# Bias lines replicated 16 times in DRAM instead of 128, and read by eight pairs of transfers onto every eighth partition

## The reference

```
s = einsum(q_blk, k) + rel_bias[rel_bucket(qpos[:, None] - kpos[None, :])]
s = where(qpos - kpos >= 0, s, -inf)
p = softmax(s)
```

## Time and profile before

| | us |
|---|---|
| median of 3 runs | 2331.86 (2328.55 to 2335.62) |
| the profiled execution | 2334.23 |
| its span | 2332.6 |
| TensorE busy | 2076.8 |
| VectorE busy | 1424.1 |
| POOL busy | 1017.5 |
| ScalarE busy | 871.6 |

### The profile page before, as it was taken

How to read it: one execution, slowest core, us unless ns; L and a number is a source line. 1 busy time by engine, 2 the same in 40 slices (tenths; PEclk the granted TensorE clock), 3 DMA queues, 4 the chain that set the end, 5 groups by cost and what they waited for, 6 DMA issues and landing times.

```text
span 2332.6 us, 24219 instructions
## 1 busy us (share of the span) xinstructions
PE 2076.8 (89%) x7378; PEld 1198.3 (51%) x7378; DVE 1424.1 (61%) x2980; ACT 871.6 (37%) x2116; POOL 1017.5 (44%) x1104
## 2 busy tenths in 40 slices
PE   7989999999999987898978998886999998878776
PEld 6768877778868643453423443342445444222222
DVE  3674464554477579774576654476846558684445
ACT  3544444645434332652223252223325223222222
POOL 0200000100000047677467566556755756777774
PEclk9999999999999899999999999998999999999999
DMA  8435545155545679999999999999999999999997
GB/s 315 171 124 174 190 161 205 50 190 180 180 145 185 271 319 409 344 396 412 414 410 409 416 411 412 411 414 396 401 415 387 413 413 409 410 409 409 409 410 310
DMA packets 172558, 752.66 MB, mean 323 GB/s; under 512 B 19184, under 2 KB 19472, under 8 KB 152864
## 3 DMA queue, kind: packets, MB, share of 16 engines
q0 software_dynamic: 148640, 544.05, 58.9%
q1 hardware_dynamic: 22224, 198.37, 22.7%
q10 hardware_dynamic: 1584, 8.91, 1.0%
HBM read 750.18 MB, written 4.22 MB: 323 GB/s over the span
## 4 chain that ended last, share of the span: by engine, by line
PE 49%; DMA 19%; DVE 12%; POOL 9%; issue 8%; ACT 2%; DVEq 1%; POOLq 0%; ACTq 0%; SPq 0%
PE ps L998 13%; DMA Z<-v,experts 10%; PE ps L731 8%; PE ps L733 8%; PE ps L732 8%; DMA Z<-u,experts 7%; PE ps L1018 6%; DVE Z L2039 5%; POOL Z L2413 4%; POOL Z L2428 3%; POOL ring L2428 1%; DMA ring<-panels 1%; PE ps L1075 1%; DVE ring_lo L1850 1%; DMA ring<-v,experts 1%
## 5 line engine op out<-in xcount | busy, mean ns | idle before, releaser
L998 PE MATMUL ps<-Z 128*128 128x512 f32 x1792 | 853.7, 622 | 157.8 <-DMA Z<-v,experts 95.4
L2039 DVE CUSTOM_DVE_ANT_0 Z<-Z,ps 128x1024 f32<-128x1024 f32 x512 | 612.0, 1219 | 408.6 <-DMA Z<-u,experts 402.1
L998 PEld LDWEIGHTS ps<-Z 128*128 128x128 f32 x1792 | 335.8, 197 | 635.4 <-issue 393.6
L2413 POOL DMA_INDIRECT Z<-u,experts x512 | 489.7, 956 | 293.0 <-issue 138.1
L2428 POOL DMA_INDIRECT Z<-v,experts x448 | 430.8, 962 | 252.0 <-PE ps L998 145.9
L1850 DVE TENSOR_TENSOR ring_lo<-ring,ring_hi 128x1024 fp32r<-128x1024 f32 x212 | 247.9, 1221 | 195.8 <-ACT ring_hi L1311 195.5
L1470 ACT ACTIVATE hdot<-hdot 128x4 f32<-128x4 f32 x128 | 26.3, 205 | 655.5 <-DVE hdot L2039 655.3
L731 PE MATMUL ps<-ring_hi,xT_lo 128*128 128x512 f32 x592 | 237.9, 402 | 14.2 <-DVE xT_lo L1909 8.9
L1018 PE MATMUL ps<-ring,o 128*128 128x512 f32 x528 | 232.3, 593 | 1.4 <-ACT o L1498 1.4
L732 PE MATMUL ps<-ring_lo,xT 128*128 128x512 f32 x592 | 232.9, 393 | 0.0
L733 PE MATMUL ps<-ring_hi,xT 128*128 128x512 f32 x592 | 232.7, 393 | 0.0
(11 more groups left out here) (285 smaller groups left out, 2152.0 us busy)
## 6 DMA issues: line engine op xcount, KB each, us to landing
ring<-panels SPq DMA_DIRECT2D x106, 1024.0 KB, 5.0
ring<-panels SPq DMA_DIRECT2D x37, 2048.0 KB, 10.4
Z<-u,experts POOLq DMA_INDIRECT x512, 12.1
Z<-v,experts POOLq DMA_INDIRECT x448, 12.8
Z<-panels SPq DMA_DIRECT2D x3, 2048.0 KB, 21.8
gain<-gains ACTq DMA_DIRECT2D x4, 1024.0 KB, 4.7
bias_lines<-bias_line POOLq DMA_DIRECT2D x1, 3072.0 KB, 13.8
gain<-gains ACTq DMA_DIRECT2D x5, 512.0 KB, 6.8
```

The costliest lines, as they stand in the source:

```text
L998: last = mm(ps[:, c, :], diag[s], vrow[s][:, c * NC:(c + 1) * NC], start=slot == 0, stop=slot == SLOTS - 1 or n == SUMMED[-1] - 1)
L2039: v.tensor_tensor_reduce(out=row, in0=row, in1=dotted, scale=1.0, scalar=0.0, op0=ALU.mult, op1=ALU.add, accum_out=hdot[:, t, slot:slot + 1])\
L2413: g.indirect_dma_start(out=urow[s], out_offset=None, in_=(u0, u1)[layer], in_offset=bass.IndirectOffsetOnAxis(ap=experts[:, t, slot:slot + ...
```

## The change

The replicated tensor has 16 copies instead of 128. Eight transfers of `later` and eight of `early` take the place of one each. Transfer number `at` fills partitions at, at + 8, ..., at + 120, sixteen of them, each from a copy of its own. The start of the source moves by one element with each `at`, and by eight from one of its partitions to the next. The waits count 256 instead of 32, since each transfer adds 16.

```diff
+COPIES = 16
...
-    lines_dram = nc.dram_tensor("bias_lines", (P, HEADS, LINE), F32).ap()
+    lines_dram = nc.dram_tensor("bias_lines", (COPIES, HEADS, LINE), F32).ap()
...
                 if call == 0:
-                    dve.wait_ge(lines_in, 32)
+                    dve.wait_ge(lines_in, 2 * 16 * P // COPIES)
...
                     pool.dma_start(lines_dram.rearrange("p h l -> p (h l)"),
-                                   bass.AP(line_dram.tensor, 0, [[0, P], [1, HEADS * LINE]])).then_inc(lines_out, 16)
+                                   bass.AP(line_dram.tensor, 0, [[0, COPIES], [1, HEADS * LINE]])).then_inc(lines_out, 16)
 
                     pool.wait_ge(lines_out, 32)
-                    later = bass.AP(lines_dram.tensor, P - 1, [[HEADS * LINE - 1, P], [LINE, HEADS], [1, SEQ]])
-                    early = bass.AP(lines_dram.tensor, 2 * P - 1, [[HEADS * LINE - 1, P], [LINE, HEADS], [1, P]])
-                    pool.dma_start(bias[:, :, P:S_COLS], later).then_inc(lines_in, 16)
-                    pool.dma_start(bias[:, :, 0:P], early).then_inc(lines_in, 16)
+                    for at in range(P // COPIES):
+                        steps = [[HEADS * LINE - P // COPIES, COPIES], [LINE, HEADS]]
+                        later = bass.AP(lines_dram.tensor, P - 1 - at, steps + [[1, SEQ]])
+                        early = bass.AP(lines_dram.tensor, 2 * P - 1 - at, steps + [[1, P]])
+                        pool.dma_start(bias[at::P // COPIES, :, P:S_COLS], later).then_inc(lines_in, 16)
+                        pool.dma_start(bias[at::P // COPIES, :, 0:P], early).then_inc(lines_in, 16)
...
-                    pool.wait_ge(lines_in, 32)
+                    pool.wait_ge(lines_in, 2 * 16 * P // COPIES)
                     pool.wait_ge(loaded, 16 * 3)
```

## The result

The changed kernel takes 2336.98 us (median of 22 runs, 2329.85 to 2343.15) against 2331.44 for the kernel before on the same chip (22 runs, 2328.48 to 2337.14). Forecast were 2328 us and a range of 2322 to 2334. The time is within the 0.3% called no change, but on the other side and outside the range. The profiled execution took 2338.71 us, with a span of 2337.1.

What follows compares the result with a forecast made beforehand. TensorE is busy 89% of the span, and from 950 us gathers fill the transfer engines; the change touches only the first 80 us. Terms 0 - 4.0 + 0 + 0 + 0 = -4.0 us gave 2327.9, range 2322 to 2334.

Steps and rivals of the forecast that it cites:

- Parts 1 and 3: POOL's start: replication lands after 4.5 us, sixteen bias reads issue from 37.4 us at 0.6 us each; 0.
- Rival B: POOL's queue delays the attention if an issue costs over 1.0 us: 2334.8 (chance 0.05), or serially 2360 (0.03).
- Part 5: The two changed waits, VectorE's for the bias and POOL's before staging: bias lands by 61, 11.8 us of cover; 0.
- small row: Last small transfer behind the bias reads in POOL's queue, whose landing frees POOL to stage; POOL forecast free at 61.
- Part 2: The late panel near 48 us: its halves land in time, so hole and lower clock behind it vanish; -4.0 us.
- old hole: TensorE's 2.14 us idle before the matmul at 50.50, waiting for a late panel; 4.02 us with the clock loss.
- higher row: The longer of two profiled landing times, 8.3 and 9.8 us, of panel halves beside the bias reads.
- Part 4: Moved reads lie over panel 3's second half and panel 4, which still lands with 2.8 and 1.3 us room; 0.
- queue model: Transfer engines' work from 37.4 us: reads at 332 GB/s take 9.5 us, 21.8 in all, through by 59.2.
- rival A: Narrow reads at half rate delay panel 4: hole of 2.7 us, 4.6 with clock; +0.6, 2332.5 us; chance 0.18.

Runs made afterwards that it cites:

- byhead128: Kernel before with its 128 copies, but sixteen bias reads, each of two heads onto all 128 partitions; 2333.25 us, ratio 1.0006.
- copies32: Changed kernel with 32 copies instead of 16, four pairs of reads onto partitions 4 apart; 2331.02 us (0.9998 of before), repeated 2332.38 (1.0012).
- changed_again: The changed kernel repeated unchanged for a second trace; 2333.42 us, ratio 1.0013 to the kernel before.
- three controls: The kernel before, unchanged, traced three more times; 2330.34 us (ratio 1.0007) for the first, then one execution each of 2329.28 and 2331.59.
- copies64: Changed kernel with 64 copies instead of 16, two pairs of reads onto every second partition; 2331.01 us (0.9999 of before), repeated 2331.26 (0.9994).

## Why the prediction was wrong

**Parts 1 and 3 were right.** Replication: 3.3 us to landing against 4.5; first bias read at 36.87 against 37.4, though the engine came 0.7 late to it. Issues: 0.56 against 0.6, with some luck: the number of runs, by which the step chose, doesn't set the time alone. byhead128's reads have the same 256 runs and take 0.73 to 0.76 us to issue. Rival B's own mechanism, an issue dearer than 1.0 us, did not occur. **Part 5 was right in what releases what**, with less room than given: VectorE's score work is released by TensorE, POOL's staging by TensorE, 1.7 us after the small row's landing instead of 11.8. The landings themselves were far off: the bias was due by 61 and came at 71.3, the small row at 75.1.

**Part 2 closed the old hole, but at a price from one execution.** TensorE has no idle time at 48 to 50 us. The step's term, -4.0, was 2.1 of hole and 1.9 of clock. Over six traces of kernels with 128 copies and wide reads the excess of that panel is 4.02, 2.34, 1.76, 1.85, 2.02 and 3.88, a mean of 2.6: behind holes of 1.4 to 2.1 us the clock fell in two of six. And of panel 3's second half the step said that it lands at the higher row, 9.8; it took 11.8, which ate the 1.2 us of room and left the hole of 0.73.

**Part 4 is the step that failed:** "Panel 4's halves, at 8.3 and 9.8, land at 54.1 and 58.3", so "0". They took 11.9 and 14.7, and the sign that the prediction names for being wrong, a new hole of over 1 us before 85 us, came true. The durations came from rows in which wide reads stood beside the panels, and the queue model from 332 GB/s; both held for copies32 (8.4 and 10.1 us for panel 4's halves) and byhead128 (8.5 and 9.5), neither for reads onto partitions 8 apart. With those the engines are as busy and pass a quarter to a third less. The new hole, 2.50 us and 4.50 with the clock, is the place and nearly the size that rival A named (2.7, and 4.6). The size has luck in it: by A's own terms the halves land at 45.83 + 15.6 = 61.4, not 62.3, which makes a hole of 1.8; they landed at 64.1. A alone would have been +0.6; its chance of 0.18 was too low, since the argument against it rested on rows of another kind of read.

The rule quoted with A, the Trainium skill (SBUF — State Buffer, section "Door 1: The DMA port swizzle"), agrees with the traces in order: partitions 4 apart and whole sets, which reach all 16 ports by it, pass 363 to 370 GB/s; 8 apart, 8 ports, 242 and 272; sixteen neighbours, 4 ports, 189. The rates hold the panels' own bytes too, so they are no clean halves and quarters, and no run wrote by ports alone.

**The balance.** At the first score work the changed kernel stands, as a mean of its two traces, at 86.2 us, and the kernel before, over its four, at 83.4: +2.8. That is the mean of 5.53 and 4.94 of new holes less 2.5 of old (four traces), 2.7. Behind the fourth staged pair come 0.9 more. Together +3.7, against +3.0 (0.13%, changed_again) and +4.4 (0.19%) in the timed runs. The stretch near 770 us isn't in that sum. By the traces it is 3.0 to 6.4 us longer in the changed kernel than in the three controls, but equal to before's own; timed runs carry no such marks, and both traced executions of the changed kernel were slower than its medians (2338.71 for 2336.98, 2339.59 for 2333.42), so how much of it is in the medians stays open.

Against the forecast of -4.0 the traces thus account for 7.6 us: 5.2 for the new holes that part 4 put at 0, 1.5 by which part 2 priced the old hole too high, 0.9 for the drain, which had no term. Measured were 8.4 and 7.0.

**What the forecast would have needed** was also not to be had from the hole alone. copies32 has it closed with no new one, scores start 3.2 us sooner (80.2 for 83.4), and its times are 0.9998 and 1.0012 of before: the attention gives back 0.4, the stretch near 770 us some 3. No version here beats the kernel before; the nearest, copies64, has 0.9999 and 0.9994 (0.9985 to 1.0003).

Not tried: reading the lines directly from the single one in DRAM, which needs a source that steps backwards.

## What to carry over

When copies are thinned out and a read becomes several strided ones, see which partitions each of them writes: reads onto 32 partitions 4 apart passed as much as those onto all 128 (363 and 370 GB/s), onto 16 partitions 8 apart about two thirds to three quarters of it (242 and 272), and the neighbours in other queues paid for it. A duration "beside such reads" holds for reads onto the same partitions only. Price a hole with the clock loss behind it from several executions, and expect of a few microseconds won early that a later stretch with a clock of its own may keep them.

## What was not expected of the hardware

The share of busy transfer engines doesn't tell their rate: 1.00 stood beside 228 GB/s and 1.01 beside 410. A `drain` of POOL grew with the number of reads issued some 50 to 60 us before, 1.30, 1.47, 1.79 and 2.44 us for 2, 4, 8 and 16. And a stretch in which TensorE is 93% busy with small matmuls had a granted clock of 0.50 over 10 us in one kernel and 0.66 in another; the stretch around it took 75.9 and 81.3 us in two executions of the same kernel.
